# The four feed-forward blocks' first matrices by Strassen block products: 20 of 22 tile pairs as seven products in place of eight

## The reference, cut to what matters

```python
D_MODEL = 1024; SEQ = 512           # D_FF = 22 * 128 = 2816

def swiglu_ffn(x, wi, wo):
    gate, up = jnp.split(x @ wi, 2, axis=-1)
    return (jax.nn.silu(gate) * up) @ wo

for l in range(DEPTH_2):            # two layers
    x = layer_norm(alpha * x + 0.5 * swiglu_ffn(x, ffn1_wi[l], ffn1_wo[l]), ln_g[l, 0], ln_b[l, 0])
    ...                             # the layer's mixer and its norm
    x = layer_norm(alpha * x + 0.5 * swiglu_ffn(x, ffn2_wi[l], ffn2_wo[l]), ln_g[l, 2], ln_b[l, 2])
```

## Time and profile before

| | |
|---|---|
| timed runs | 4629.52, 4630.28, 4631.79 us |
| profiled execution | span 4631.4 us from its first to its last instruction; the profile gives no other time of its own |
| busy share of the span | TensorE 97%, its weight loads 81%, VectorE 56%, ScalarE 34%, GpSimd 32% |
| the chain that ended last | TensorE 83%, VectorE 11%, GpSimd 2%, waits for issue 1%, ScalarE 1% |
| mean granted TensorE clock | 0.975 of full speed |
| HBM | 591.78 MB read, 68.16 MB written, 142 GB/s over the span |

### The profile page before, as it was taken

How to read it: one execution, slowest core, us unless ns; L and a number is a source line. 1 busy time by engine, 2 the same in 40 slices (tenths; PEclk the granted TensorE clock), 3 DMA queues, 4 the chain that set the end, 5 groups by cost and what they waited for, 6 DMA issues and landing times.

```text
span 4631.4 us, 55643 instructions
## 1 busy us (share of the span) xinstructions
PE 4481.6 (97%) x22359; PEld 3731.9 (81%) x22359; DVE 2611.0 (56%) x3691; ACT 1574.0 (34%) x2177; POOL 1487.1 (32%) x961
## 2 busy tenths in 40 slices
PE   7999999999999999999999999999999999999998
PEld 4757855779989999999888876788788878887887
DVE  4756667469869988788622355422322256554223
ACT  3334211233335543333322255322322243223222
POOL 2042024206877658778411100210211101123111
...
GB/s 174 51 150 96 142 61 66 82 83 180 255 236 217 262 328 394 373 384 388 226 96 96 91 75 45 78 96 96 82 96 93 94 83 76 24 33 64 96 96 73
DMA packets 228968, 663.58 MB, mean 143 GB/s; under 512 B 22039, under 2 KB 87975, under 8 KB 226536
## 3 DMA queue, kind: packets, MB, share of 16 engines
...
HBM read 591.78 MB, written 68.16 MB: 142 GB/s over the span
## 4 chain that ended last, share of the span: by engine, by line
PE 83%; DVE 11%; POOL 2%; issue 1%; ACT 1%; DMA 1%; DVEq 0%; ACTq 0%; POOLq 0%; SPq 0%
PE ps L257 21%; PE ps L258 20%; PE ps L259 20%; PE ps L1536 2%; DVE r L226 2%; DVE A L1965 2%; PE ps L584 2%; PE ps L1615 1%; DVE A L2264 1%; PE ps L3363 1%; PE ps L3370 1%; DVE A L2265 1%; PE ps L268 1%; PE ps L389 1%; POOL r L226 1%
## 5 line engine op out<-in xcount | busy, mean ns | idle before, releaser
L257 PE MATMUL ps<-r,r 128*128 128x512 f32 (+2 forms) x5160 | 1933.2, 375 | 18.8 <-POOL r L226 13.7
L258 PE MATMUL ps<-r,r 128*128 128x512 f32 (+2 forms) x5160 | 1915.8, 371 | 0.0
L259 PE MATMUL ps<-r,r 128*128 128x512 f32 (+2 forms) x5160 | 1915.6, 371 | 0.0
L226 DVE TENSOR_TENSOR r<-A,r 128x1024 fp32r<-128x1024 f32 x588 | 789.3, 1343 | 1416.7 <-ACT r L220 1409.6
L220 ACT ACTIVATE r<-A 128x1024 fp32r<-128x1024 f32 x665 | 704.1, 1059 | 1741.7 <-PE ps L259 1558.8
L257 PEld LDWEIGHTS ps<-r,r 128*128 128x128 f32 x5160 | 974.5, 189 | 166.6 <-issue 19.3
L258 PEld LDWEIGHTS ps<-r,r 128*128 128x128 f32 x5160 | 974.6, 189 | 136.2 <-issue 3.4
L259 PEld LDWEIGHTS ps<-r,r 128*128 128x128 f32 x5160 | 973.7, 189 | 135.1
L276 POOL TENSOR_TENSOR r<-A,r 128x512 fp32r<-128x512 f32 (+2 forms) x303 | 403.3, 1336 | 1355.6 <-ACT r L273 1220.7
L273 ACT ACTIVATE r<-A 128x512 fp32r<-128x512 f32 (+1 forms) x264 | 150.6, 579 | 434.6 <-DVE A L2338 249.3
L226 POOL TENSOR_TENSOR r<-A,r 128x1024 fp32r<-128x1024 f32 x77 | 206.6, 2686 | 160.0 <-ACT r L220 159.1
...
## 6 DMA issues: line engine op xcount, KB each, us to landing
A<-in_pu SPq DMA_DIRECT2D x128, 512.0 KB
A<-in_pv SPq DMA_DIRECT2D x128, 512.0 KB
...
acts<-A ACTq DMA_DIRECT2D x128, 192.0 KB
...
```

The lines of the kernel that those rows point to most:

```text
L226: e.tensor_tensor(self.vr(at + 1024, 1024), self.v(self.st0 + 1024 * (u % RS), 1024), self.vr(at, 1024).bitcast(F32), ALU.subtract).then_i ...
L257: t.matmul(o, hi, xh, start=first and k == k0, stop=False)
L258: t.matmul(o, hi, xl, start=False, stop=False)
L259: m = t.matmul(o, lo, xh, start=False, stop=final and k == K - 1)
```

## The change

In a pair, the weights of gate and up (128 outputs each) and the two halves of the contraction (k-tiles 0 to 3 and 4 to 7) form a 2 x 2 block matrix, and so do the halves of the contraction and of the tokens (256 columns each) on the other side. After the change, pairs 2 to 21 of each block (`PAIRS = 20`) are computed as seven products of such blocks, with summed operands on both sides (Winograd's form of Strassen's method), each of 4 k-tiles x 3 matmuls x 256 columns. The first two pairs stay as they were.

- The stream holds only the four units of the first two pairs, four pauses and the second matrix. The raw tiles of the other 20 pairs are loaded by `ffn_s` itself, two pairs deep.
- Sums of weights: four a pair, by GpSimd (`sum_g`). Sums of tokens: four of 128 x 1024 a block, by VectorE (`token_v`), split in hi and lo (`token_a`, `token_lo_v`).
- Operands: seven of 128 x 512 a pair, hi by ScalarE (`operand_a`), lo by VectorE (`operand_v`), in a ring of 11 places.
- Results: products 11 and 12 add up in bank A, s2, s3 and 22 in bank B, s1 and s4 in bank C. ScalarE copies product 11 ("one") out before 12 is added; VectorE makes five additions with PSUM as an input (`quarter_v`).
- silu works on 256 columns at a time out of PSUM and SBUF; the multiplication by up moves from VectorE to GpSimd (`gated`).
- The hidden tiles' parts are made late, when room is free, by tables of places (`LATE_A`, `LATE_V`).
- The `after` waits at the start of each engine's part of a block go.

The order of the products is 11, then 22 of the pair before, s2, s1, 12, s3, s4.

```diff
-    out += [("f1i0", 0, 44), ("f1o0", 0, 22), ("ev", 0, 8), ...
+    layer = lambda n, l: [(f"f{n}i{l}", 0, 4), ("pause", 0, 4), (f"f{n}o{l}", 0, 22)]
...
+    def product_t(self, t, i, p, x):
+        bank = {"11": "A", "12": "A", "s2": "B", "s3": "B", "22": "B", "s1": "C", "s4": "C"}[x]
+        opens = x in ("11", "s2", "s1")
+        ps = self.bank_t(t, bank, i, p) if opens else self.ps(bank, i, p)
+        if x in ("12", "s3", "22", "s4"):
+            t.wait_ge(*S.at({"12": "one", "s3": "one six", "22": "lower right", "s4": "one five"}[x], i, p))
+        if p == 0 and x in ("s1", "s2", "s3", "22"):
+            t.wait_ge(*S.at("token lo", i, x))
+        t.wait_ge(*S.at("part lo", i, p, x))
+        at = self.slot(i, L.nth[p, x])
+        for k in range(4):
+            hi, lo = ...
+            xh, xl = self.tokens(x, k)
+            t.matmul(ps[:, 0:256], hi, xh, start=opens and k == 0, stop=False, ...)
+            t.matmul(ps[:, 0:256], hi, xl, start=False, stop=False, ...)
+            m = t.matmul(ps[:, 0:256], lo, xh, start=False, stop=k == 3, ...)
+        m.then_inc(*S.on("t", "product", i, p, x))
...
     def ffn_t(self, t, i, tag):
         self.group_pair(t, outs, hr, [(x, i, 0) for x in ("gate", "up")], [("nlo", tag, k) for k in range(8)])
-        for f in range(1, 22):
+        for x in ("gate", "up"):
+            ps = self.bank_t(t, x, i, 1)
+            self.group(t, [ps[:, :]], [hr], 8, x, i, 1)
+        self.cur["t"] += 32
+        for p, x in L.seven:
+            self.product_t(t, i, p, x)
...
+    def ffn_a(self, a, i, parts):
+        for f in range(2):
+            if f == 0:
+                self.weights_a(a, 32)
             a.wait_ge(*S.at("gate", i, f))
+            a.activation(self.v(L.HID + 512 * f, 512), self.ps("gate", i, f)[:, :], ACT.Silu)...
+            if f == 0:
+                self.token_a(a, i, "s1")
+                self.operand_a(a, i, 0)
+                self.token_a(a, i, "s2")
+                self.token_a(a, i, "s3")
+                for n in range(1, 3):
+                    self.operand_a(a, i, n)
+        for n in range(3, 7):
+            self.operand_a(a, i, n)
+        self.token_a(a, i, "22")
+        for n in range(7, 11):
+            self.operand_a(a, i, n)
+        for m, (p, x) in enumerate(L.seven):
+            if x == "11":
+                ...                                     # copy "one", silu of the right half of p - 1
+            if x == "12":
+                self.gate_half_a(a, i, p, 0)
+            self.operand_a(a, i, m + 11)
+            for f in self.LATE_A.get(m, ()):
+                self.hidden_a(a, i, f)
...
+    def ffn_v(self, v, i, tag, parts):
+        self.weights_v(v, 32)
+        v.wait_ge(*S.at("whole", tag, 7))
+        for x in ("s1", "s2", "s3"):
+            self.token_v(v, i, x)
+        self.times_up_v(v, i, 0)
+        self.operand_v(v, i, 0)
+        self.token_lo_v(v, i, "s2")
+        self.operand_v(v, i, 1)
+        self.token_lo_v(v, i, "s1")
+        self.operand_v(v, i, 2)
+        self.token_v(v, i, "22")
+        self.operand_v(v, i, 3)
+        self.token_lo_v(v, i, "s3")
+        self.times_up_v(v, i, 1)
+        for n in range(4, 7):
+            self.operand_v(v, i, n)
+        self.token_lo_v(v, i, "22")
+        for n in range(7, 10):
+            self.operand_v(v, i, n)
+        for m, (p, x) in enumerate(L.seven):
+            self.quarter_v(v, i, p, x)
+            self.operand_v(v, i, m + 10)
+            for f in self.LATE_V.get(m, ()):
+                self.hidden_lo(v, "v", i, f)
...
+    def sum_g(self, g, i, p, x):
+        one, two, how = {"s1": (up, up + 512, ALU.add), "s3": (gate, up, ALU.subtract), "s2": (up + 512, up, ALU.subtract), "s4": (gate + 512, L.SB + 512, ALU.subtract)}[x]
+        if x == "s1":
+            for half in range(2):
+                g.wait_ge(*S.at("raw", i, p, half))
+        ...
+        if p and x != "s3":
+            g.wait_ge(*S.at("part lo", i, p - 1, x))
+        ...
+    def ffn_g(self, g, i, parts):
+        for p in range(self.PAIRS):
+            for x in ("s1", "s3", "s2"):
+                self.sum_g(g, i, p, x)
+            if p >= 2:
+                self.gated(g, "g", i, p - 2)
+            self.sum_g(g, i, p, "s4")
```

More of the change, by code:

```diff
@@ new lines, in lay_ffn, with raw_at, raw_gone @@
+        for i, banks in ((1, (1, 2, 5)), (4, (4, 5, 2))):
+            self.plan([("back", i, o) for o in range(8)], banks)
+    def raw_at(self, i, p, half):
+        j = 2 * (p % 2) + half
+        r = self.L4.u0[i] + (0, 2, 1, 0)[j]
+        return (self.L4.RX, "stx") if j == 0 else (self.st0 + 1024 * (r % RS), f"st{r % RS}")
+    def raw_gone(self, e, i, p, half):
+        S = self.S
+        e.wait_ge(*S.at("part lo", i, p, ("12", "22")[half]))
+        e.wait_ge(*S.at("sum", i, p, ("s4", "s2")[half]))
@@ L2550, in ffn_t @@
+    def ffn_t(self, t, i, tag):
         S, L = self.S, self.L4
@@ L2560, in ffn_t, with operand_a @@
+        self.cur["t"] += 32
+        for p, x in L.seven:
+            self.product_t(t, i, p, x)
+        hidden = lambda k: (self.vr(L.HI[k], 512), self.vr(L.HID + 512 * k, 512))
+        self.back_t(t, i, hidden, 22, [("hidden lo", i, k) for k in range(22)], L.WK)
         self.end("t", ("ffn", i))
[L2562 removed]
+    def operand_a(self, a, i, n):
         S, L = self.S, self.L4
[L2564 to L2574 removed]
+        if n >= len(L.seven):
+            return
+        p, x = L.seven[n]
+        if n >= 11:
+            a.wait_ge(*S.at("product", i, *L.seven[n - 11]))
+        elif n >= 5:
+            a.wait_ge(*S.at("used", L.u0[i] + (1, 3, 2)[(n - 5) // 2]))
+        if x in ("11", "12", "22"):
+            a.wait_ge(*S.at("raw", i, p, int(x == "22")))
+        else:
+            a.wait_ge(*S.at("sum", i, p, x))
+        self.part_hi(a, self.operand(i, p, x), self.slot(i, n), 512, "part hi", i, p, x)
@@ new lines, in token_a, with gate_half_a @@
+    def token_a(self, a, i, x):
+        S = self.S
+        raw, less, hi, lo = self.token_sums(x)
+        a.wait_ge(*S.at("token sum", i, x))
+        if x == "22":
+            a.wait_ge(*S.at("up", i, 1))
+        a.activation(hi, raw, ACT.Copy).then_inc(*S.on("a", "token hi", i, x))
+    def gate_half_a(self, a, i, p, right):
+        S, L = self.S, self.L4
+        h = self.v(L.HID + 512 * (p + 2) + 256 * right, 256)
+        if right:
+            a.wait_ge(*S.at("upper right", i, p))
+            a.activation(h, self.v(L.E + 256 * (p % 2), 256), ACT.Silu).then_inc(*S.on("a", "silu", i, p, 1))
+        else:
+            a.wait_ge(*S.at("product", i, p, "12"))
+            a.activation(h, self.ps("A", i, p)[:, 0:256], ACT.Silu).then_inc(*S.on("a", "silu", i, p, 0))
+            S.mark("a", "out", "A", i, p)
@@ L2577, in ffn_a, with operand_v @@
         self.end("a", ("ffn", i))
-    def ffn_v(self, v, i, prior, parts):
+    def operand_v(self, v, i, n):
         S, L = self.S, self.L4
-        self.after(v, "v", prior)
-        for f in range(22):
-            tm = self.v(L.TM + 512 * (f % 2), 512)
-            self.weights_v(v, 8)
-            self.weights_v(v, 8)
-            v.wait_ge(*S.at("out", "gate", i, f))
-            v.wait_ge(*S.at("up", i, f))
-            v.tensor_tensor(tm, tm, self.ps("up", i, f)[:, :], ALU.mult).then_inc(*S.on("v", "out", "up", i, f))
+        if n >= len(L.seven):
+            return
+        p, x = L.seven[n]
+        v.wait_ge(*S.at("part hi", i, p, x))
+        at = self.slot(i, n)
+        self.part_lo(v, "v", self.operand(i, p, x), at, at + 512, 512, "part lo", i, p, x)
@@ new lines, in token_v, with token_lo_v @@
+    def token_v(self, v, i, x):
+        S = self.S
+        raw, (one, two), hi, lo = self.token_sums(x)
+        if x in ("s2", "22"):
+            v.wait_ge(*S.at("token sum", i, {"s2": "s1", "22": "s2"}[x]))
+        v.tensor_tensor(raw, one, two, ALU.subtract).then_inc(*S.on("v", "token sum", i, x))
+    def token_lo_v(self, v, i, x):
+        S = self.S
+        raw, less, hi, lo = self.token_sums(x)
+        v.wait_ge(*S.at("token hi", i, x))
+        v.tensor_tensor(lo, raw, hi.bitcast(F32), ALU.subtract).then_inc(*S.on("v", "token lo", i, x))
@@ new lines, in gated, with hidden_lo @@
+    def gated(self, e, who, i, p):
+        S, L = self.S, self.L4
+        h = self.v(L.HID + 512 * (p + 2), 512)
+        e.wait_ge(*S.at("lower left", i, p))
+        for right in range(2):
+            e.wait_ge(*S.at("silu", i, p, right))
+        e.tensor_tensor(h, h, self.v(L.CU + 512 * (p % 2), 512), ALU.mult).then_inc(*S.on(who, "hidden", i, p + 2))
+    def hidden_lo(self, e, who, i, f):
+        S, L = self.S, self.L4
+        e.wait_ge(*S.at("hidden hi", i, f))
+        self.part_lo(e, who, self.v(L.HID + 512 * f, 512), L.HI[f], L.HID + 512 * f, 512, "hidden lo", i, f)
@@ L3859, in chain_t @@
         self.cur["t"] += 24
-        self.back_t(t, 4, N.HR, 8, None, N.NW, start=3)
+        self.back_t(t, 4, self.pair(N.HR, 8), 8, None, N.NW, start=3)
```

248 lines of the change are left out of this document (189 added, 59 removed).

## The result

| | median us | lowest to highest | runs | ratio to before |
|---|---|---|---|---|
| before | 4631.42 | 4627.06 to 4636.87 | 11 | |
| after | 4624.92 | 4611.69 to 4629.98 | 11 | 0.9978 [0.9969, 0.9986] |

The change saves 6.5 us, 0.22%, with an interval of 0.14 to 0.31%. The forecast was 4619 and faster. The profiled execution of after has a span of 4625.9 us at a mean clock of 0.970, against 4631.4 us at 0.975.

What follows compares the result with a forecast made beforehand. TensorE, busy for 97%, was taken to bound the kernel. A block: 14.0 us to the fifth product, 204.2 for 19.43 pairs, 2.0 for clock and end, 220.2 against 223.1; 11.6 saved in all, 4619 us, range 4568 to 4655.

Steps and rivals of the forecast that it cites:

- TensorE's part: In a changed pair, 84 matmuls of 256 columns at 0.1188 us each take 9.98 us, against 11.155 before.
- The turns: In a steady pair, VectorE's low parts and GpSimd's operations alternate at a shared port, 0.55 + 1.13 us a turn: 10.5 us.
- rival 1: TensorE sets the pair at 9.98 to 10.05 us, saving 13.2 us a block: 4577 us; chance 0.27.
- the wait of s4's low part and the fixed trigger: In a pair, s4's low part waits behind `gated`, itself started by "lower left"; argued against a 9.98 to 10.05 us pair.
- The start: At each block's start, TensorE pauses 5.1 and 3.1 us, so the fifth product comes 14.0 us after the first.
- The raw tiles are there in time: At a block's start, raw weight loads, asked 6 us or more ahead, hold nothing up; first pair up to 1 us late.
- The clock: Behind the second starting pause, products run at half clock, 2.6 us instead of 1.4: 1.5 us a block, 0 to 4.
- The sum: Each feed-forward block takes 220.2 us against 223.1: 2.9 us saved a block, 11.6 in all.
- The end of a block: At the second matrix, late hidden tiles are nearly all ready in time: 0.5 us a block, 0 to 3.
- other stages: unchanged: Outside the changed blocks, the second matrix, norms and other stages keep their time.
- Rival 2: The port sets the pair, with no overlap at a hand-over: 11.1 us a pair, 4665 us; chance 0.18.
- Rival 3: TensorE stays longer at half clock after the pauses, or block ends aren't hidden: 3 us more a block, 4630; chance 0.07.

Runs made afterwards that it cites:

- e10: e2 with matmuls that nobody reads in the block's two starting pauses, 7 before product 12 and 1 before s3 of pair 0; 4589.99 us, 0.9910 of before.
- e1: After with GpSimd's weight sums cut to 16 of 512 columns from pair 1 on, same order and waits; 4576.58 us in a single run.
- e2: The swap: after with GpSimd's sum s4 placed ahead of `gated` of two pairs before, instead of behind it; 4589.16 us, 0.9899 of before.
- e5: After with `gated` (gate x up) of pairs 0 to 17 on VectorE instead of GpSimd; 4593.65 us, 0.9925 of before.
- e11: The same kernel as e2, run once more to see how much it varies; 4586.39 us, 0.9897 of before.
- e9: e2 with matmuls that nobody reads at the block's start, 11 before product 12 and 7 before s3 of pair 0; 4608.48 us, 0.9956 of before.
- e0: The unchanged kernel before, run again for a second profile; 4634.73 us in a single run.
- e3: After with pair 0's first three VectorE additions and ScalarE's copy "one" moved ahead of other work; 4623.31 us, 0.9977 of before.
- e8: e2 plus the early additions and copy of e3, and operand 7 ahead of 5 and 6 on ScalarE and VectorE; 4591.50 us, 0.9904 of before.

## Why the prediction was right, and where it wasn't

**TensorE's part** (0.1188 us a matmul, 9.98 a pair): right. The swapped kernel, in which TensorE doesn't pause, has a pair of 10.00, and 9.99 in e10.

**The turns** (0.55 and 1.13; pair 10.5): right, 10.51 in each of the four blocks. The steps of the cycle stand in the steady pair above: `gated` at 0 (2399.55), lo(s3) ends at 2.34 (forecast 2.3), VectorE then idle until ScalarE has s4's high part, lo(s4), 1.03 us long from 2403.79, ends at 5.27 (5.25), GpSimd idle for 2.49 us (2.4). That VectorE's and GpSimd's operations take turns is seen in the durations, 1.45 us for a low part that takes 0.68 alone. e1 shows that the pair hangs on the time GpSimd's sums take (10.06 with short ones), and e2 that it takes the tie of s4 to "lower left" as well (with all the work but without the tie 10.0); e5 agrees. The prediction named this tie ("the wait of s4's low part and the fixed trigger") as what spoke against rival 1, and didn't ask whether an edit could remove it. The Trainium skill, "SBUF — State Buffer", section "Who interferes with whom", has each of the two hold the port for its whole instruction. The lock is there. But by the whole durations a pair needs 11.1 us of it, and e2 runs the same operations in 10.0: the hand-over costs less than both durations in full, and here the measurement decides.

**The means of the low parts and sums**: about 1.0 and above 1.5 forecast, 1.072 and 1.607 measured.

```profile
L277 DVE TENSOR_TENSOR r<-A,r 128x512 fp32r<-128x512 f32 x645 | 676.5, 1072 | 126.4 <-ACT r L274 122.6
...
L2882 POOL TENSOR_TENSOR A<-A 128x512 f32<-128x512 f32 x320 | 511.6, 1607 | 63.2 <-DVE r L277 33.7
```

**The start** (fifth product 14.0 us after the first, pauses of 5.1 and 3.1): the sum right, its parts not. The fifth product came at 2327.20, 13.9 us after 2313.28. The pauses were 5.99 and 0.53 us: the first was 0.9 longer than forecast, and product 12, between them, ran at half clock and took 2.9 us for 1.4; the forecast had the half clock only behind the second pause. VectorE's "one six" ended at 2327.15, forecast 2326.2, and the first product had begun 1.1 us later than the forecast 2312.2, so that the two shifts cancel. "The raw tiles are there in time" was wrong: once a block GpSimd's sums wait 5.2 to 5.5 us for one, which the prediction had named as a sign that its forecast would be wrong. That wait lies behind the fifth product, in a part that the prediction took to be steady.

**The clock** (1.5 us a block, 0 to 4): mis-sized. In the swapped kernel full clock at the start is worth 0.3 to 1.6 us a block, 2.7 us in all (e10 against e11), since VectorE, not TensorE, sets the place of the fifth product, and product 12's extra 1.4 us are in its shadow. The products of the first block were nevertheless 220.7 us long (220.3 and the last three matmuls), forecast 220.2 with clock and end in it. "Lower left" came 22.4 us after the first product, and from there 19 pairs of 10.51: what was put down to the clock lies in the first pair. There the high part that VectorE waits for begins at 2333.80, and GpSimd's sums, late by the raw tile, end at 2333.71. So full clock could have moved it by 0.1 us at the most, and the nearly exact total is in part luck: a wait that was left out stands where too much was put down to the clock. A run of the unswapped kernel at full clock, which would show it directly, was not made.

**The sum** (11.6 us): 11.0 in the four blocks, or 13.6 against the second profile of before. The end of a block was hidden as forecast: no wait of the second matrix for a hidden tile is in the list of waits.

**What was missing.** The forecast was 11.6 us off the median and 6.5 were measured. The term that failed is "other stages: unchanged". The odd layer's mixer was 4.4 us longer in the profile. Both kernels run the same 3288 matmuls there. The whole stage in the view of windows, and under it 25 us from the same place of it, 275 us behind its start, before and then after:

```profile
3714.00:4240.80 526.80, 505.53 (x3288) 420.60 (x3288) 287.52 (x395) 163.21 (x248) 94.35 (x67) 0.94 0.15 54
...
3989.00:4014.00 25.00, 25.00 (x162) 21.50 (x161) 5.10 (x8) 6.14 (x12) 0.00 (x0) 0.93 0.08 24
```

```profile
3706.30:4237.60 531.30, 510.67 (x3288) 424.54 (x3288) 288.19 (x395) 163.23 (x248) 93.94 (x67) 0.93 0.16 54
...
3981.30:4006.30 25.00, 25.00 (x135) 21.19 (x134) 2.99 (x5) 5.54 (x11) 0.00 (x0) 0.75 0.00 1
```

TensorE's idle time is no longer (21.3 and 20.6 us); the same matmuls are busy for 5.1 us more. In the slice the clock is 0.75 in place of 0.93, and 135 matmuls fall into it in place of 162. Of the 21 slices of 25 us, 17 agree within 0.01, and the three others that differ do so by +0.14, −0.02 and −0.04. Over all kernels the stage's length follows its mean clock: what the 21 slices lack of full clock comes to 29.5 us in e9 (524.4 long), 31.2 in before and e0 (526.9, 527.0), 33.0 in e1, e3, e5 and e10 (530.1 to 530.4), 33.8 in after (531.3) and 35.5 to 35.8 in e2, e8 and e11 (531.7 to 531.8). So the 4.4 us are clock and not work. Whether the change brings them isn't settled. The stage's code is the same, and e9, with changed blocks, is shorter than before. But both profiles of the kernel before have the same length, and seven of the eight other kernels are longer by 3 to 5 us, so it isn't chance from run to run in these profiles either. What decides where the clock falls stays open.

The timed runs of after hang on the clock too: they spread over 18 us, with a mean clock of 0.974 in the two of 4612 us and 0.969 to 0.971 in those above 4622. A difference of 6.5 us between medians is less than the 7.4 us by which this one stage differs between kernels.

**The rivals.** Rival 1 (TensorE sets the pace, 13.2 us a block, 4577) is not what the change does, but nearly what it does once s4 stands elsewhere: the blocks of e11 are 368.9, 370.1, 371.3 and 365.7 us long, 11.8, 12.8, 10.4 and 11.4 less than before's, 46.4 us in all. Rival 2 (no overlap, 11.1 a pair) is excluded by 10.51 in all four blocks. Rival 3's place was right (half clock behind the pauses) and its size small.

**The better version** is the swap, e2 and e11: 1.0% faster than before and 0.8% faster than after.
